# Two layers with a product-key expert network: looked-up expert rows against all experts from streamed tables

## The reference

```python
h  = rms_norm(x, norm1_g) * (1 + sc1) + sh1      # sh, sc, g from silu(cond) @ ada_w + ada_b
p  = h @ w_in                                    # 1024 x 2560: three groups of mixers
x += g1 * (concat(gqa(p), diff_attention(p), short_conv(p)) @ w_out)
h  = rms_norm(x, norm2_g) * (1 + sc2) + sh2
x += g2 * peer_ffn(h, peer_wq, peer_keys, peer_u, peer_v)

def peer_ffn(h, wq, sub_keys, u_tab, v_tab):     # 8 heads, 128 keys a half, 16384 experts
    q  = (h @ wq).reshape(P_CHUNK, 8, 2, 128)
    sc = einsum('thcd,hcnd->thcn', q, sub_keys)
    s1, i1 = top_k(sc[:, :, 0], 16); s2, i2 = top_k(sc[:, :, 1], 16)
    top_s, pos = top_k(s1[..., :, None] + s2[..., None, :], 16)   # of the 256 pairs
    eidx = take(i1 * 128 + i2, pos); gate = softmax(top_s)
    act  = gelu(einsum('thkd,td->thk', u_tab[eidx], h))
    return einsum('thk,thkd->td', gate * act, v_tab[eidx])
```

## Time and profile before

| | us |
|---|---|
| median of three timed executions | 3092.7 |
| lowest and highest of them | 3091.23, 3098.33 |
| span of the profiled execution | 3171.0 |
| TensorE, VectorE, GpSimd, ScalarE busy in it | 2487.3, 1897.5, 1712.9, 550.0 |

### The profile page before, as it was taken

One profiled execution on the slowest core, in us unless ns is written; L12 is line 12 of the kernel. 1 busy time (PEld: TensorE's weight loads), 2 busy tenths in 40 slices (PEclk: granted clock), 3 DMA queues, 4 the chain that ended last, 5 costly groups with the idle time before them and its releaser, 6 DMA issues.

```text
span 3171.0 us, 27910 instructions
## 1 busy us (share of the span) xinstructions
PE 2487.3 (78%) x6500; PEld 1148.6 (36%) x6500; DVE 1897.5 (60%) x5815; ACT 550.0 (17%) x1600; POOL 1712.9 (54%) x1588
## 2 busy tenths in 40 slices
PE   7875888788979888767788896789966766666667
PEld 1244333345623233323354343444732222222222
DVE  0044367873475657768757538784366777477664
ACT  0121112222111111112211112332111111111111
POOL 0002445443366667667667544463346777577675
PEclk9867899888989989888889798888988888778888
DMA  8526787667889999989999787776768999789888
GB/s 293 198 94 239 282 285 275 236 241 266 300 319 401 402 403 401 368 299 343 359 378 396 247 307 255 262 285 223 274 222 323 360 351 337 293 325 339 320 327 303
DMA packets 298730, 961.85 MB, mean 303 GB/s; under 512 B 28304, under 2 KB 30736, under 8 KB 297840
## 3 DMA queue, kind: packets, MB, share of 16 engines
q0 software_dynamic: 221184, 805.40, 69.5%
q1 hardware_dynamic: 77328, 154.96, 13.6%
q10 hardware_dynamic: 96, 0.10, 0.0%
HBM read 957.63 MB, written 2.62 MB: 303 GB/s over the span
## 4 chain that ended last, share of the span: by engine, by line
PE 39%; DVE 29%; issue 14%; DMA 9%; POOL 3%; ACT 2%; another core or an unknown queue 2%; DVEq 0%; POOLq 0%; SPq 0%; ACTq 0%
PE ps_acc L785 17%; DVE u_ring L1309 10%; PE ps_mm L610 5%; PE ps_mm L751 5%; DMA u_ring<-peer_u,gathered 4%; PE ps_mm L571 3%; PE ps_mm L723 2%; DMA v_ring<-peer_v,gathered 2%; POOL u_ring L517 2%; DMA weights<-ada_w 2%; POOL v_ring L517 2%; PE ps_mm L664 1%; DVE half_idx L1262 1%; DVE half_top L1258 1%
## 5 line engine op out<-in xcount | busy, mean ns | idle before, releaser
L785 PE MATMUL ps_acc<-v_ring,diag 128*128 128x512 f32 x3072 | 1536.5, 654 | 452.4 <-ACT diag L979 249.0
L517 POOL DMA_INDIRECT u_ring<-peer_u,gathered x768 | 836.3, 1089 | 795.0 <-DVE dots L1309 466.9
L785 PEld LDWEIGHTS ps_acc<-v_ring,diag 128*128 128x128 f32 x3072 | 626.6, 211 | 1279.1 <-issue 1052.5
L517 POOL DMA_INDIRECT v_ring<-peer_v,gathered x768 | 861.3, 1121 | 339.8 <-issue 216.0
L1309 DVE CUSTOM_DVE_ANT_0 u_ring<-u_ring,h 128x1024 f32<-128x1024 f32 x768 | 908.3, 1221 | 71.9 <-DMA u_ring<-peer_u,gathered 68.3
L979 ACT ACTIVATE diag<-consts,coef 128x128 f32<-128x128 f32 x768 | 245.6, 390 | 150.3 <-DVE coef L1323 87.0
L610 PE MATMUL ps_mm<-weights,hT 128*128 128x512 f32 x480 | 213.4, 598 | 2.9 <-DMA weights<-w_in 1.8
L1321 DVE TENSOR_SCALAR gexp<-gexp 128x4 f32<-128x4 f32 x192 | 41.6, 217 | 282.3 <-ACT gexp L973 216.0
L973 ACT ACTIVATE gexp<-poly 128x4 f32<-128x4 f32 x192 | 39.3, 205 | 891.8 <-DVE poly L1318 658.3
L751 PE MATMUL ps_mm<-hT,weights 128*128 128x128 f32 (+1 forms) x1024 | 182.6, 332 | 9.2 <-issue 8.6
L571 PE MATMUL ps_mm<-weights,condT 128*2 128x512 f32 x384 | 172.4, 605 | 18.3 <-DMA weights<-ada_w 18.3
(11 more groups left out here) (184 smaller groups left out, 1820.4 us busy)
## 6 DMA issues: line engine op xcount, KB each, us to landing
weights<-ada_w SPq DMA_DIRECT2D x24, 2048.0 KB
weights<-w_in SPq DMA_DIRECT2D x20, 2048.0 KB
weights<-peer_wq SPq DMA_DIRECT2D x16, 2048.0 KB
weights<-w_out SPq DMA_DIRECT2D x8, 2048.0 KB
u_ring<-peer_u,gathered POOLq DMA_INDIRECT x768
v_ring<-peer_v,gathered POOLq DMA_INDIRECT x768
weights<-peer_keys SPq DMA_DIRECT2D x4, 1024.0 KB
par<-params SPq DMA_DIRECT2D x2, 1026.0 KB
```

Of the source, the lines that this page charges most:

```text
L517: pool.indirect_dma_start(ring[:, slot, :], None, table, bass.IndirectOffsetOnAxis(ap=gathered[:, p, at:at + 1], axis=0)).then_inc(full[sl ...
L785: last = pe.matmul(ps_acc[:, b * NB:(b + 1) * NB], diag[:, slot, :], v_ring[:, slot, b * NB:(b + 1) * NB], start=False, stop=False)
```

## The change

The row lookups go, and with them GpSimd's indirect DMAs, the dot products on VectorE, the diagonal matrices and `Beside`. The host lays the tables out in 128 blocks a layer. Block j holds the experts whose second key is j, one for each first key, and SP streams it: 512 KB of `peer_u` (transposed) and 512 KB of `peer_v` into rings of four that lie over `weights`. For every block TensorE computes the pre-activations of 128 experts for all 384 tokens (`before_gelu`: 8 products of 384 columns), ScalarE and VectorE apply the gelu (a tanh) and multiply with a gate, and TensorE adds the block to the sums of the three tiles (`add_block`: 6 products of 512 columns), which stay in three pairs of PSUM banks.

The gate of a token for all 16384 experts is a 128x128 matrix, the sum over its 128 picks of (one-hot of the first key) x (one-hot of the second key, times half the softmax weight). It is one product per token (`open_gates`): VectorE writes the first one-hot rows for four tokens at a time (`first_rows`), GpSimd the second ones, a token each, TensorE multiplies, ScalarE copies four tokens out into `stage`, and SP stores 32 tokens at a time (2 MB) to memory outside the core and loads them back by blocks of 8 (`load_gates`). `route` now ranks the 8 heads of a tile together, in place, and yields between its instructions.

The order: `modulate(0)`; then for each layer the prompt's dense stages, the sample's, the next layer's modulation, the gates of the three tiles, and all the experts. On VectorE the prompt tile is ranked in steps between the sample's dense stages, tile 1 after them, tile 2 between `first_rows(l, 0)` and `first_rows(l, 1)`. The second norm's transposed output goes to `hT2`, which the query products and the experts read. The main parts:

```diff
+            def store_gates(l, i):
+                sp.wait_ge(outer_read, (l * TGROUPS + i + 1) * TG // TOK)
+                sp.dma_start(gates_hbm[i], stage[:, i % 2].rearrange("p j n -> p (j n)")).then_inc(gates_stored[i % 2], 16)
+            def load_gates(l, c):
+                n = GCHUNK * TG
+                if c < 2:
+                    for i in range(2):
+                        sp.wait_ge(gates_stored[i], (l + 1) * TGROUPS // 2 * 16)
+                else:
+                    sp.wait_ge(gates_used, l * BLOCKS + (c - 1) * GCHUNK)
+                sp.dma_start(gates[:, c % 2].rearrange("p (g n) -> p g n", g=TGROUPS),
+                             gates_hbm.rearrange("g p n -> p g n")[:, :, c * n:(c + 1) * n]).then_inc(gates_full[c % 2], 16)
+            def table_block(l, j):
+                if j >= URING:
+                    sp.wait_ge(pre_mm, l * BLOCKS + j - URING + 1)
+                elif j == 0:
+                    last = first_chunk(l + 1) + ADA_CHUNKS if l + 1 < DEPTH else DEPTH * LAYER_CHUNKS
+                    for c in (last - 2, last - 1):
+                        sp.wait_ge(*used(c))
+                sp.dma_start(u_ring[:, j % URING].rearrange("p k e -> p (k e)"), peer_u[l, j]).then_inc(u_full[j % URING], 16)
+                if j >= VRING:
+                    sp.wait_ge(block_done, l * BLOCKS + j - VRING + 1)
+                sp.dma_start(v_ring[:, j % VRING], peer_v[l, j]).then_inc(v_full[j % VRING], 16)
...
+            ada_chunks(0)
             for l in range(DEPTH):
...
                 group_chunks(l, P_TILES)
                 group_chunks(l, S_TILES)
+                if l + 1 < DEPTH:
+                    ada_chunks(l + 1)
+                for j in range(URING):
+                    table_block(l, j)
+                for i in range(TGROUPS):
+                    store_gates(l, i)
+                for c in range(2):
+                    load_gates(l, c)
+                for j in range(URING, BLOCKS):
+                    table_block(l, j)
+                    c = (j - 5) // GCHUNK + 1
+                    if j % GCHUNK == 5 and 2 <= c < BLOCKS // GCHUNK:
+                        load_gates(l, c)
...
         @block.gpsimd
...
+            for l in range(DEPTH):
+                for t in range(T):
+                    n = l * T + t
+                    pool.wait_ge(picksT_ready, n + 1)
+                    for g in range(GROUPS):
+                        i = n * GROUPS + g
+                        if i >= 2:
+                            pool.wait_ge(outer_mm, i - 1)
+                        for q in range(TOK):
+                            at = g * TOK + q
+                            last = pool.tensor_scalar(onehot[:, 1, i % 2, q, :], iota128, picksT[:, n % 2, 1, at:at + 1],
+                                                      picksT[:, n % 2, 2, at:at + 1], ALU.is_equal, ALU.mult)
+                        last.then_inc(second_ready, 1)
...
         @block.tensor
...
+            def open_gates(l, t):
+                n = l * T + t
+                pe.wait_ge(picks_ready, n + 1)
+                if t == 0:
+                    pe.wait_ge(ps_ready, group_nth(l, S_TILES, 15, 16))
+                else:
+                    pe.wait_ge(picksT_ready, n)
+                for c in range(3):
+                    last = pe.transpose(ps_tr[:, c * P:(c + 1) * P], picks[:, t, c, :], ident)
+                last.then_inc(picksT_mm, 1)
+                for g in range(GROUPS):
+                    i = n * GROUPS + g
+                    pe.wait_ge(first_ready, i + 1)
+                    pe.wait_ge(second_ready, i + 1)
+                    if i >= 4:
+                        pe.wait_ge(outer_read, i - 3)
+                    for q in range(TOK):
+                        last = pe.matmul(outer(i)[:, q, :], onehot[:, 0, i % 2, q, :], onehot[:, 1, i % 2, q, :], start=True, stop=True)
+                    last.then_inc(outer_mm, 1)
+            def experts(l):
+                def before_gelu(j):
+                    pe.wait_ge(u_full[j % URING], (l * BLOCKS // URING + j // URING + 1) * 16)
+                    if j >= 2:
+                        pe.wait_ge(pre_read, l * BLOCKS + j - 1)
+                    for k in range(KC):
+                        last = pe.matmul(mm(j, NT), u_ring[:, j % URING, k, :], hT2[:, k, :], start=(k == 0), stop=(k == KC - 1))
+                    last.then_inc(pre_mm, 1)
+                def add_block(j):
+                    pe.wait_ge(v_full[j % VRING], (l * BLOCKS // VRING + j // VRING + 1) * 16)
+                    pe.wait_ge(coef_ready, l * BLOCKS + j + 1)
+                    for t in range(T):
+                        for b in range(2):
+                            last = pe.matmul(sums[t][:, b * NB:(b + 1) * NB], coef[:, j % 3, t * P:(t + 1) * P],
+                                             v_ring[:, j % VRING, b * NB:(b + 1) * NB], start=(j == 0), stop=(j == BLOCKS - 1))
+                    last.then_inc(block_done, 1)
+                pe.wait_ge(mod_staged, min(l + 2, DEPTH) * ADA_CHUNKS)
+                before_gelu(0)
+                pe.wait_ge(outer_read, (l + 1) * T * GROUPS)
+                for j in range(BLOCKS):
+                    if j + 1 < BLOCKS:
+                        before_gelu(j + 1)
+                    add_block(j)
+                pe.wait_ge(pre_read, (l + 1) * BLOCKS)
+                broadcast(ps_mm[:], l, 0, GATE2).then_inc(gate2_bc, 1)
+                pe.wait_ge(x_fed, l * T + 1)
+                broadcast(ps_mm[:], l, 1, GATE2).then_inc(gate2_bc, 1)
...
         @block.scalar
...
+            def open_gates(l, t):
+                n = l * T + t
+                act.wait_ge(picksT_mm, n + 1)
+                act.activation(picksT[:, n % 2], ps_tr[:, 0:3 * P].rearrange("p (c n) -> p c n", c=3), ACT.Copy).then_inc(picksT_ready, 1)
+                for g in range(GROUPS):
+                    i = n * GROUPS + g
+                    part, at = i * TOK // TG, i * TOK % TG
+                    if at == 0 and part >= 2:
+                        act.wait_ge(gates_stored[part % 2], part // 2 * 16)
+                    act.wait_ge(outer_mm, i + 1)
+                    act.activation(stage[:, part % 2, :, at:at + TOK].rearrange("p j n -> p n j"), outer(i),
+                                   ACT.Copy).then_inc(outer_read, 1)
+            def experts(l):
+                for j in range(BLOCKS):
+                    act.wait_ge(pre_mm, l * BLOCKS + j + 1)
+                    if j >= 2:
+                        act.wait_ge(coef_ready, l * BLOCKS + j - 1)
+                    act.activation(pre[:, j % 2], mm(j, NT), ACT.Square).then_inc(square_ready, 1)
+                    act.wait_ge(z_ready, l * BLOCKS + j + 1)
+                    act.activation(pre[:, j % 2], pre[:, j % 2], ACT.Tanh, scale=GELU_B).then_inc(tanh_ready, 1)
+                act.wait_ge(block_done, (l + 1) * BLOCKS)
+                for t in range(T):
+                    act.activation(summed[:, t], sums[t][:], ACT.Copy).then_inc(sum_copied, 1)
...
         @block.vector
...
+            def route(l, t):
...
+                for lo in (0, 8):
+                    for h, c in halves:
+                        yield
+                        last = dve.max(half_top[:, h, c, lo:lo + 8], half(h, c))
+                    step.after(last)
+                    for h, c in halves:
+                        yield
+                        last = dve.max_index(half_idx[:, h, c, lo:lo + 8], half_top[:, h, c, lo:lo + 8], half(h, c))
+                        if lo == 0:
+                            last = dve.match_replace(half(h, c), half_top[:, h, c, 0:8], half(h, c), NEG)
+                    step.after(last)
...
+            def first_rows(l, t):
+                n = l * T + t
+                dve.wait_ge(picksT_ready, n + 1)
+                for g in range(GROUPS):
+                    i = n * GROUPS + g
+                    if i >= 2:
+                        dve.wait_ge(outer_mm, i - 1)
+                    to = onehot[:, 0, i % 2]
+                    dve.tensor_tensor(to, iota128.unsqueeze(1).broadcast_to(to.shape),
+                                      picksT[:, n % 2, 0, g * TOK:(g + 1) * TOK].unsqueeze(2).broadcast_to(to.shape),
+                                      ALU.is_equal).then_inc(first_ready, 1)
+            def experts(l):
+                for j in range(BLOCKS):
+                    n, c = l * BLOCKS + j, j // GCHUNK
+                    dve.wait_ge(square_ready, n + 1)
+                    z = pre[:, j % 2]
+                    step.after(dve.tensor_scalar(z, z, GELU_A, 1.0, ALU.mult, ALU.add))
+                    dve.tensor_tensor(z, z, mm(j, NT), ALU.mult).then_inc(z_ready, 1)
+                    if j % GCHUNK == 0:
+                        dve.wait_ge(gates_full[c % 2], (l * BLOCKS // GCHUNK // 2 + c // 2 + 1) * 16)
+                    gate = gates[:, c % 2].rearrange("p (g j n) -> p j g n", g=TGROUPS, j=GCHUNK)[:, j % GCHUNK]
```

(79 more changed lines are left out.)

563 lines of the change are left out of this document (181 added, 382 removed).

## The result

The changed kernel takes 4828.2 us (median of four executions, 4823.76 to 4833.63), the kernel before 3092.9 (3091.23 to 3098.33) on the same chip. The ratio is 1.560, 95% interval 1.558 to 1.563. The forecast was 4600, with a range of 4330 to 4960. The side was right, the time lies in the range, and the number was 5% low. The price of the experts' products, which decides the side, was right; the gates, whose groups take 3.54 us and not 2.2, were not. Nearly all of the difference lies there.

A forecast was written before the change was run, and what follows sets the result against it. The prediction saw three engines taking turns, TensorE busiest at 78%; after the change, 113 + 336 + 750 + 94 + 54 + 108 + 440 + 36 + 2641 + 28 gave 4600 us, range 4330 to 4960.

The forecast's parts named there:

- TensorE's price per column: Experts: time proportional to columns, 0.322 us for 384 and 0.429 for 512, two instructions a product; 10.31 us a block, 2639 us.
- Rival D: Experts: matmuls overlap in the array, so tables set a block at 3.8 us; 2940 us in all, chance 0.02.
- The elementwise chain: Experts: six gelu and gate operations, none above 0.62 us, with two table loads 6.3 us a block, hidden under TensorE's 10.31.
- Rival B: Experts: the elementwise chain sets a block; at 12.6 us a block 5190 us in all, chance 0.03.
- Rival C: Experts: TensorE's clock does not hold at 1.00; at a mean of 0.9, 4890 us in all, chance 0.04.
- The order of stages: Dense stages, modulation and rankings no longer lie beside experts: 113 + 336 + 750 + 94 + 108 us exposed, plus transfers of 36.
- The gates: Building gates before the experts: GpSimd sets a group of four tokens at 2.2 us, 192 groups, 440 us with openings.
- the prediction's own sign of being wrong: Stated test: prediction wrong if a block is far from 10.3 us, or the gates' group is over 3.5 us.
- the forecast's case: Blocks at 10.3 us and a group of gates between 0.9 and 3.3 us; chance 0.78.
- rival A: Gates: GpSimd is the bound by far, its tensor_scalar costing 0.94 us like its DMA issue; 5030 us in all, chance 0.13.
- The hold-up by VectorE: Gates: first_rows' comparison with two SBUF inputs delays GpSimd by its whole 0.69 us a group, on top of 1.5.
- the profile's 2.5%: Whole kernel before: timed median 2.5% below the profiled 3171.0 us span; forecast left it out, allowing part in the low end.

The follow-up runs named there:

- experiment 4: Changed kernel with half of the contraction of the pre-activations left out (4 of 8 products of 384 columns a block): 4174.1 us.
- experiment 7: On top of experiment 3, the experts' tables, activations and coefficients cast to bf16 on the chip, sums still f32: 2747.6 us, ratio 0.888.
- experiment 1: Changed kernel with half of the second one-hot rows left out (GpSimd makes two of four a group): 4486.6 us.
- experiment 3: Changed kernel with the second one-hot rows made by VectorE after its comparison, GpSimd doing nothing: 4462.9 us.
- experiment 5: Changed kernel with GpSimd's tensor_scalar over 32 of the 128 elements, in the same number: 4612.9 us.
- Experiment 2: Changed kernel with the comparison of first_rows reading its keys from PSUM, so VectorE has one SBUF input instead of two: 4739.4 us.

## Why the prediction was right, and where it was off

**TensorE's price per column: right.** The step from weight loads 0.429 us apart to 10.31 us a block is met to the hundredth, and experiment 4 shows that it scales with the columns. The experts are 55% of the time after, and this term decided the direction. Rival D (products overlap, tables set a block) is refuted by the block of 10.31 us in f32. An instruction of 512 columns takes 0.429 us in f32 and 0.215 in bf16 (experiment 7).

**The elementwise chain: right, and cheaper than bounded.** The six operations are 0.36 to 0.56 us, and the blocks have no table load. Rival B is out: experiment 4 ran at 7.73 us a block, and experiment 7 at 3.61 with casts added. Rival C, a clock under 1.00, didn't come either, over two stretches of 1300 us.

**The order of stages: right.** To the first norm 115 (113 forecast), the prompt group 167 (168), the sample group 372 (375), layer 1's modulation 97 (94), a ranking about 55 (54), store and gate load 17.6 and 16 (18). The scaling of pieces of a stage that never ran alone held within 1%.

**The gates: the step that failed.** I forecast 440 us. They take 343 a layer (751 to 860 and 915 to 1149, and the same in layer 1), 685 in all: 245 too many, where the whole sum was 227 short; the other terms together were 18 too high. The prediction read: "A write of 128 elements is nearer the copy: I take 0.38". GpSimd's tensor_scalar takes 0.787, so four of them cost 3.15 and not 1.5 us a group: 192 x 1.63 = 313 more. Experiments 1, 3 and 5 show it as the bound and its size. By the prediction's own sign of being wrong, a group over 3.5 us, it was wrong here: a group is 3.54, where 2.2 was forecast, and it lies between the forecast's case (0.9 to 3.3) and rival A (4.45). The time stays in the range because the range's high end had room for a group at 3.5, not because this step held. The row that I leaned on, a copy of 16 elements in 0.20 us, has one input and an eighth of the elements; by experiment 5 even 32 elements of this operation cost 0.466. Rival A, GpSimd as the bound of the gates by far, was the better account, though with 0.94 us it was too high as well: of the 202 us between its 5030 and the 4828 measured, 0.94 against 0.787 makes 118, the full 0.69 for the hold-up 58, and the other terms the rest.

**The hold-up by VectorE: right in kind, too large.** I added the comparison's whole 0.69 us. Experiment 2 gives 0.44 to 0.46 by removing it. By the rest of a group over four medians it is 0.39, that is 58 us less than forecast, and this error hid part of the first by luck. With one of the comparison's two inputs in PSUM the hold-up is gone (a group of 3.10 us for four operations of 0.776).

**What I left out.** ScalarE's copy into `stage`, whose neighbours lie 32 floats apart, takes 1.05 us and not the 0.60 of a plain copy (no run changed the distance alone), and TensorE's clock in the gates is 0.50, so that its eight instructions take 2.05 us and not 0.90. Both are hidden under GpSimd's 3.15. The low end that I gave a group, TensorE's 0.9, was too low even at a clock of 0.91: its eight instructions take 1.13 us in experiment 1, and with GpSimd out of the way 1.63 is what VectorE allows. The allowance for the profile's 2.5% was not needed.

## What to carry to other kernels

Before lookups are replaced by dense products, work out TensorE's time from the columns and the type: in f32 the experts' sum was 2640 us, against 3093 for the whole kernel with lookups. The 450 us between them are used up by the modulation and the two projections alone (1056 instructions of 512 columns at 0.429 us, an estimated 453 us on TensorE), so that no better schedule of the rest could win it back. In bf16 the same products cost a quarter (0.215 us for 512 columns instead of twice 0.429), and with the one-hot rows on VectorE the change comes out 11% ahead of the f32 kernel before. An operation that the trace doesn't show, 768 times on the only path of a stage, deserves the pessimistic end of its bounds, and the engine that has the slack deserves the work: VectorE did the same four rows in 1.10 us. Where short GpSimd operations set the pace, look at what VectorE reads beside them: moving one of its two inputs to PSUM took 89 us off here.

## What the runs showed of the hardware

- GpSimd's tensor_scalar with two pointer scalars, f32: 0.466 us for 32 elements a partition, 0.787 for 128. VectorE: 0.275 apiece in a row of four.
- A VectorE comparison of 0.69 us with two SBUF inputs cost GpSimd 0.44 us in each group of 3.54; with one input in PSUM, nothing: a group was 3.10 us. Beside four two-input operations of 2.28 us ten of GpSimd's took 17.16 us instead of some 7.9.
- TensorE's granted clock: 0.50 where a group's products came every 3.54 us, 0.91 to 0.98 where the same products came every 1.63 to 1.76 us (experiments 1 and 3). So in these gates the slow partner also came with a slower TensorE: 2.05 us for the eight instructions instead of 1.13.
- ScalarE's copy of 512 elements from PSUM to places 128 bytes apart: 1.05 us, against 0.60 for the one to adjacent places in the earlier trace rows.
- VectorE's cast of 1024 elements from f32 to bf16 took 0.69 us, as long as an f32 comparison of 512; a comparison in bf16 with broadcast inputs took 679 ns, and 682 in f32. Which of its operands keeps it slow was not tried.
